# Turning blocks without TensorE: VectorE 32x32 transposes and GpSimd block copies in a hybrid attention layer

## The reference

```
h = rms_norm(x); proj = h @ w_in
retention (4 heads):      scores = (q k^T) * decay; o = scores v + (q * decay) (state from the chunk before)
gated delta rule (6):     short convolution, l2 norm, chunked triangular solve
attention (6 heads):      q, k normalised; softmax(q k^T - slope * distance) v, causal
y = concat over heads of rms_norm(o) * silu(gate)   (attention: o * silu(gate))
out = x + y @ w_out
```

## Time and profile before

| | before |
|---|---|
| median of 3 runs | 522.1 us (521.22 to 522.24) |
| profiled execution | 521.48 us |
| its span | 519.7 us |
| PE busy | 513.7 us (99%) |
| PEld (weight loads) | 431.3 us (83%) |
| DVE busy | 337.0 us (65%) |
| ACT busy | 277.0 us (53%) |
| POOL busy | 91.7 us (18%) |
| granted TensorE clock | 1.00 throughout |

### The profile page before, as it was taken

The page is one execution under the profiler, slowest core; times in us unless marked ns, Lnnn a source line. Parts: engine busy times, 40 slices in busy tenths (PEclk is TensorE's granted clock), DMA queues, the critical chain, the costliest instruction groups (busy, mean ns, idle before and its releaser), DMA issues.

```text
span 519.7 us, 8821 instructions
## 1 busy us (share of the span) xinstructions
PE 513.7 (99%) x3496; PEld 431.3 (83%) x3496; DVE 337.0 (65%) x529; ACT 277.0 (53%) x439; POOL 91.7 (18%) x84
## 2 busy tenths in 40 slices
PE   8999999999999999999999999999999999999996
PEld 6888888888888888888888888888888888888885
DVE  3999999989765876664644554655366455646551
ACT  5777645654356676565535554664556456443340
POOL 4764253316131312110000000100010010000000
PEclk9999999999999999999999999999999999999999
DMA  8999655765744466576676577657765557758711
GB/s 281 311 293 238 165 138 149 193 154 147 197 124 125 124 160 155 131 202 163 162 186 179 131 212 189 171 160 191 188 178 163 164 158 223 220 177 226 247 40 41
DMA packets 146923, 91.68 MB, mean 176 GB/s; under 512 B 7907, under 2 KB 135874, under 8 KB 146882
## 3 DMA queue, kind: packets, MB, share of 16 engines
q1 hardware_dynamic: 143392, 88.94, 63.0%
q10 hardware_dynamic: 3490, 2.18, 1.5%
HBM read 89.00 MB, written 2.10 MB: 175 GB/s over the span
## 4 chain that ended last, share of the span: by engine, by line
PE 97%; DVE 2%; ACT 0%; issue 0%; POOL 0%; DVEq 0%; POOLq 0%
PE pj L1450 20%; PE pj L1449 20%; PE pj L1447 20%; PE pj L1425 13%; PE pj L1426 6%; PE pj L1495 3%; PE pj L1504 1%; PE mx L1593 1%; PE pj L1422 1%; PE mx L1644 1%; DVE w_lo L353 1%; PE mx L1626 1%; PE mx L1474 1%; PE mx L1714 1%; PE pj L1512 1%; PE mx L1702 1%
## 5 line engine op out<-in xcount | busy, mean ns | idle before, releaser
L353 DVE TENSOR_TENSOR w_lo<-w_raw,w_hi 128x1024 fp32r<-128x1024 f32 x160 | 199.8, 1255 | 92.8 <-ACT w_hi L451 92.5
L451 ACT ACTIVATE w_hi<-w_raw 128x1024 fp32r<-128x1024 f32 x159 | 167.7, 1058 | 135.2 <-PE pj L1450 113.6
L1447 PE MATMUL pj<-w_hi,hT 128*128 128x512 f32 x320 | 127.4, 398 | 0.0
L1449 PE MATMUL pj<-w_hi,hT 128*128 128x512 f32 x320 | 125.9, 393 | 0.0
L1450 PE MATMUL pj<-w_lo,hT 128*128 128x512 f32 x320 | 124.9, 390 | 0.0
L1425 PE MATMUL pj<-hT,w_hi 128*128 128x512 f32 x300 | 109.3, 404 | 0.2 <-DVE w_lo L353 0.2
L1426 PE MATMUL pj<-hT,w_lo 128*128 128x256 f32 x300 | 83.9, 280 | 0.0
L1450 PEld LDWEIGHTS pj<-w_lo,hT 128*128 128x128 f32 x320 | 60.1, 188 | 12.4
L1447 PEld LDWEIGHTS pj<-w_hi,hT 128*128 128x128 f32 x320 | 60.1, 188 | 11.8
L1449 PEld LDWEIGHTS pj<-w_hi,hT 128*128 128x128 f32 x320 | 60.2, 188 | 11.3
L1425 PEld LDWEIGHTS pj<-hT,w_hi 128*128 128x128 f32 x300 | 56.3, 188 | 14.3 <-DVE w_lo L353 1.6
(11 more groups left out here) (241 smaller groups left out, 507.2 us busy)
## 6 DMA issues: line engine op xcount, KB each, us to landing
w_raw<-in_w_in_dram SPq DMA_DIRECT2D x256, 256.0 KB, 3.4
w_raw<-in_w_out_dram SPq DMA_DIRECT2D x64, 256.0 KB, 4.0
big<-in_x_dram SPq DMA_DIRECT2D x9, 256.0 KB, 5.5
out_dram<-sq ACTq DMA_DIRECT2D x7, 256.0 KB, 5.7
big<-in_x_dram SPq DMA_DIRECT2D x3, 512.0 KB, 7.2
cst<-table_dram SPq DMA_DIRECT2D x1, 682.0 KB, 9.8
big<-in_x_dram SPq DMA_DIRECT2D x2, 128.0 KB, 2.6
out_dram<-sq ACTq DMA_DIRECT2D x1, 128.0 KB, 2.4
```

What stands on the lines that cost most here:

```text
L353: eng.tensor_tensor(w_lo[:, n % NSPLIT, :], w_raw[:, n % NRAW, :], w_hi[:, n % NSPLIT, :].bitcast(F32), ALU.subtract).then_inc(S("lo"), 1)
L451: act.activation(w_hi[:, n % NSPLIT, :], w_raw[:, n % NRAW, :], ACT.Copy).then_inc(S("hi_done"), 1)
L1447: ins = pe.matmul(bank[:, :], src[:, kc, 0, tok], hi[:, k, :], start=first, stop=False)
L1449: pe.matmul(bank[:, :], src[:, kc, 1, tok], hi[:, k, :], start=False, stop=False)
```

## The change

The PE transposes of retention's k and q, of attention's q and of the output rows are removed (attention's keys and the gated delta rule's stay on PE). In their place a 128x512 tile is turned in two steps. DVE's transpose turns every 32x32 block where it stands; then POOL moves the blocks between the four 32-partition bands, by `move_blocks`: 16 copies of 32 partitions x (4 x 32) elements, in four groups of four, with a wait for all copies so far between groups. The temporary tiles `turned`, `spread` and `k_turned` lie in `mT`, which nobody reads any more. `r_kT`, `r_qT`, `m_qT` and `otr` count the last group's four copies. Retention's positions behind the turning move: `gram` from 14 to 42, `s1` 20 to 47, `o` 28 to 54, `out` 52 to 78. The splits of the output rows stand 20 (ACT) and 22 (DVE) units behind `out` where they stood two, and read `spread` in SBUF where they read PSUM. Three waits and counters are renamed (`m_nrm`, `m_alibi` become `m_step`).

```diff
-U_RET = {"tr": 6, "gram": 14, "s1": 20, "o": 28, "out": 52}
-U_MOBA = {"qtr": 5, "ktr": 26, "score": 34, "pt": 54, "o": 62, "out": 72}
+U_RET = {"gram": 42, "s1": 47, "o": 54, "out": 78}
+U_MOBA = {"ktr": 26, "score": 34, "pt": 54, "o": 62, "out": 72}
@@ ACT
-                advance(U["tr"] + 2)
-                act.wait_ge(S("r_tr"), j + 1)
-                act.activation(qT, mx[0][:, :], ACT.Copy).then_inc(S("r_qT"), 1)
...
-                advance(U["qtr"] + 2)
-                act.wait_ge(S("m_qtr"), j + 1)
-                act.activation(qT, mx[3][:, :], ACT.Copy).then_inc(S("m_qT"), 1)
...
-                advance(U["out"] + 2)
+                advance(U["out"] + 20)
@@ POOL
+            def spread_rows(p):
+                pool.wait_ge(S("y_turned"), p + 1 - FIRST_ROWS)
+                if p > FIRST_ROWS:
+                    pool.wait_ge(S("yt_lo"), p - FIRST_ROWS)
+                move_blocks(spread, turned, "otr")
+
+            def move_blocks(dst, src, done):
+
+                for d in range(4):
+                    if d:
+                        pool.wait_ge(S("moved"), moved[0])
+                    for q in range(4):
+                        a, i = q * QUART, (q ^ d) * QUART
+                        ins = pool.tensor_copy(dst[i:i + QUART, :, a:a + QUART], src[a:a + QUART, :, i:i + QUART])
+                        if d < 3:
+                            ins.then_inc(S("moved"), 1)
+                            moved[0] += 1
+                        else:
+                            ins.then_inc(S(done), 1)
...
                 power(64, 80, 8).then_inc(S("m_pow"), 1)
+                pool.wait_ge(S("m_pow"), j + 1)
+                pool.wait_ge(S("m_qtr"), j + 1)
+                pool.wait_ge(S("o_psum"), p)
+                move_blocks(four(qT), turned, "m_qT")
...
                 elif kind == "ret":
+                    pool.wait_ge(S("o_psum"), p)
+                    pool.wait_ge(S("y_lo"), GDN // 2)
+                    pool.wait_ge(S("r_tr"), 2 * j + 1)
+                    move_blocks(four(kT), k_turned, "r_kT")
+                    pool.wait_ge(S("r_tr"), 2 * j + 2)
+                    move_blocks(four(qT), turned, "r_qT")
                     rms_power(p)
+                    spread_rows(p)
                 else:
                     mix_moba(p, j, 128 * (p + 1))
+                    spread_rows(p)
@@ DVE
+            def turn_rows(p):
+                dve.wait_ge(S("on"), p + 1)
+                if p > FIRST_ROWS:
+                    dve.wait_ge(S("otr"), FIRST_ROWS + 4 * (p - FIRST_ROWS))
+                dve.transpose(turned.rearrange("p n c -> p (n c)"), on[:, :, :, :].rearrange("p h c e -> p (h c e)")).then_inc(S("y_turned"), 1)
...
-                advance(U["tr"] + 2)
-                dve.wait_ge(S("r_tr"), j + 1)
-                dve.tensor_copy(kT, mx[1][:, :]).then_inc(S("r_kT"), 1)
+                advance(base + 2)
+                dve.wait_ge(S("ev_done"), TOK_EV + in_rows(p))
+                if p > FIRST_ROWS:
+                    dve.wait_ge(S("otr"), FIRST_ROWS + 4 * (p - FIRST_ROWS))
+                for i, dst in ((1, k_turned), (0, turned)):
+                    dve.transpose(dst, both[:, :, i, :]).then_inc(S("r_tr"), 1)
...
                 dve.tensor_scalar(sm[:, 80:88], sm[:, 118:126], 1.0 / P, EPS, ALU.mult, ALU.add).then_inc(S("m_norm"), 1)
+                dve.wait_ge(S("otr"), FIRST_ROWS + 4 * (p - FIRST_ROWS))
+                dve.transpose(turned, both[:, :, 0, :]).then_inc(S("m_qtr"), 1)
                 gate(p)
...
-                advance(U["out"] + 2)
+                turn_rows(p)
+                advance(U["out"] + 22)
@@ PE
-                for i, bank in ((1, mx[1]), (0, mx[0])):
-                    for n in range(4):
-                        ins = pe.transpose(bank[:, n * P:(n + 1) * P], rows[n // 2][:, n % 2, i, :], ident)
-                ins.then_inc(S("r_tr"), 1)
-                stream(U["gram"])
-                pe.wait_ge(S("r_qT"), j + 1)
-                pe.wait_ge(S("r_kT"), j + 1)
+                pe.wait_ge(S("r_kT"), 4 * j + 4)
+                pe.wait_ge(S("r_qT"), 4 * j + 4)
...
-                for n in range(4):
-                    ins = pe.transpose(mx[3][:, n * P:(n + 1) * P], rows[n // 2][:, n % 2, 0, :], ident)
-                ins.then_inc(S("m_qtr"), 1)
...
-                pe.wait_ge(S("m_qT"), j + 1)
+                pe.wait_ge(S("m_qT"), 4 * j + 4)
...
-                stream(U["out"])
-                out_transposes(p, mx[3])
```

More of the change, by code:

```diff
@@ L272, in layer @@
         rows = [both[:, 2 * h:2 * h + 2] for h in range(2)]
+        FIRST_ROWS = GDN // 2
+        turned = mT[:, 0:4, :]
+        spread = mT[:, 4:8, :]
+        k_turned = mT[:, 8:12, :]
         kT = kq[:, 0].rearrange("p c k t -> p (c k t)")
@@ L720, in split_rows @@
             def split_rows(p, y0, scales):
-                act.wait_ge(S("otr"), p + 1)
+                act.wait_ge(S("otr"), FIRST_ROWS + 4 * (p + 1 - FIRST_ROWS))
                 if len(scales) == 1:
-                    act.activation(yT[:, y0:y0 + 2, 0, :], mx[3][:, :].rearrange("p (h t) -> p h t", h=2), ACT.Copy,
+                    act.activation(yT[:, y0:y0 + 2, 0, :], spread.rearrange("p (h c) t -> p h (c t)", h=2), ACT.Copy,
                                    scale=scales[0]).then_inc(S("yt_hi"), 2)
@@ L727, in split_rows @@
                     for h in range(2):
-                        act.activation(yT[:, y0 + h, 0, :], mx[3][:, h * T:(h + 1) * T], ACT.Copy, scale=scales[h]).then_inc(S("yt_hi"), 1)
+                        act.activation(yT[:, y0 + h, 0, :], spread[:, 2 * h:2 * h + 2, :].rearrange("p c t -> p (c t)"), ACT.Copy, scale=scales[h]).then_inc(S("yt_hi"), 1)
             def mix_ret(p, j, base):
@@ L858, in advance @@
                 pos[0] = max(pos[0], u)
+            def spread_rows(p):
[3 more added lines that the diff above has]
+                move_blocks(spread, turned, "otr")
+            moved = [0]
+            def move_blocks(dst, src, done):
[10 more added lines that the diff above has]
+                            ins.then_inc(S(done), 1)
             def rms_power(p):
@@ L1244, in split_rows @@
                 if len(scales) == 1:
-                    dve.scalar_tensor_tensor(yT[:, y0:y0 + 2, 1, :], mx[3][:, :].rearrange("p (h t) -> p h t", h=2), scales[0],
+                    dve.scalar_tensor_tensor(yT[:, y0:y0 + 2, 1, :], spread.rearrange("p (h c) t -> p h (c t)", h=2), scales[0],
                                              yT[:, y0:y0 + 2, 0, :].bitcast(F32), ALU.mult, ALU.subtract).then_inc(S("yt_lo"), 1)
@@ L1248, in split_rows @@
                     for h in range(2):
-                        ins = dve.scalar_tensor_tensor(yT[:, y0 + h, 1, :], mx[3][:, h * T:(h + 1) * T], scales[h],
+                        ins = dve.scalar_tensor_tensor(yT[:, y0 + h, 1, :], spread[:, 2 * h:2 * h + 2, :].rearrange("p c t -> p (c t)"), scales[h],
                                                        yT[:, y0 + h, 0, :].bitcast(F32), ALU.mult, ALU.subtract)
@@ L1283, in mix_moba @@
                     dve.wait_ge(S("m_sq"), 2 * j + h + 1)
-                    dve.tensor_reduce(sm[:, 118 + 4 * h:122 + 4 * h], sq[:, h].rearrange("p c k t -> p (c k) t"), AX.X, ALU.add).then_inc(S("m_nrm"), 1)
-                dve.wait_ge(S("m_nrm"), 2 * j + 2)
+                    dve.tensor_reduce(sm[:, 118 + 4 * h:122 + 4 * h], sq[:, h].rearrange("p c k t -> p (c k) t"), AX.X, ALU.add).then_inc(S("m_step"), 1)
+                dve.wait_ge(S("m_step"), 4 * j + 2)
                 dve.tensor_scalar(sm[:, 80:88], sm[:, 118:126], 1.0 / P, EPS, ALU.mult, ALU.add).then_inc(S("m_norm"), 1)
+                dve.wait_ge(S("otr"), FIRST_ROWS + 4 * (p - FIRST_ROWS))
+                dve.transpose(turned, both[:, :, 0, :]).then_inc(S("m_qtr"), 1)
                 gate(p)
@@ L1296, in mix_moba @@
                     dve.wait_ge(S("m_lg"), 4 * j + 2 * h + 2)
-                    dve.scalar_tensor_tensor(lg[:, h, :], cst[:, K_DIST:K_DIST + 3 * P], slope, lg[:, h, :], ALU.mult, ALU.add).then_inc(S("m_alibi"), 1)
-                    dve.wait_ge(S("m_alibi"), 2 * j + h + 1)
+                    dve.scalar_tensor_tensor(lg[:, h, :], cst[:, K_DIST:K_DIST + 3 * P], slope, lg[:, h, :], ALU.mult, ALU.add).then_inc(S("m_step"), 1)
+                    dve.wait_ge(S("m_step"), 4 * j + h + 3)
                     for c in range(C):
@@ L1719, in mix_ret @@
                 after_gdn = PAIRS[p - 1][0] == "gdn"
-                stream(U["tr"])
+                stream(U["gram"])
                 pe.wait_ge(S("ev_done"), TOK_EV + in_rows(p))
@@ L1755, in mix_moba @@
                 pt = [kT, qT]
-                stream(U["qtr"])
+                stream(U["ktr"])
                 pe.wait_ge(S("ev_done"), TOK_EV + in_rows(p))
                 pe.wait_ge(S("yt_lo"), p - GDN // 2)
-                for n in range(4):
-                    ins = pe.transpose(mx[3][:, n * P:(n + 1) * P], rows[n // 2][:, n % 2, 0, :], ident)
```

(2 more changed lines are left out.)

## The result

| | before | after |
|---|---|---|
| median | 522.17 us (4 runs) | 538.85 us (4 runs) |
| ratio to before | | 1.0323 (95%: 1.0298 to 1.0348) |
| profiled execution, its span | 521.48, 519.7 us | 539.85, 538.1 us |
| mean granted TensorE clock | 1.000 | 0.981 |
| POOL busy | 91.7 us | 180.2 us |

A forecast was written before the change was run, and what follows sets the result against it. PE was taken to bound the kernel, 99% busy and waiting for nobody: 521.5 - 5.3 us of transposes + 0.9 of attention's waits = 517.1 us profiled, 517.7 for the median; range 515.8 to 534.

The forecast's parts named there:

- What bounds the kernel, and what PE gets back: All changed stages: PE bounds the time, and removing its transposes gives 5.3 us if no wait arises.
- ACT and DVE cost nothing; the output rows are hidden: Weight splits and output moves: DVE's 9 us more is covered by the splits' lead; output moves hide behind weight matmuls.
- Do the four copies of a group overlap?: POOL's moves: with overlap a group takes 0.53 us and a move of 16 copies 2.1; without, 4.0 us.
- What a POOL copy costs: Each copy in POOL's moves: 0.37 us as recorded, 0.23 us start to start, 0.39 at the upper end.
- the rival in a row: POOL's moves: copies one after the other, behind w_lo where due; 6.7 us slower, 528.8; chance 0.26 for 523 to 535.
- POOL and DVE shut each other out: POOL against DVE: a w_lo (1.2 us) and a POOL operation that meet run one after the other.
- Retention's room: Retention's k and q before gram: 10.4 us of room, 4.2 for w_lo, 6.2 for POOL; 2.0 to spare with overlap.
- Attention's q: Attention's q before score: 5.9 us needed of 6.3 with overlap; 0.3 us a pair charged, 0.9 in all.
- what would show it: PE's waits and POOL's timeline: right if four copies within 0.6 us; wrong if gram or score wait microseconds for POOL.

The follow-up runs named there:

- The output rows alone: The changed kernel with retention's and attention's turning back on TensorE at the old positions, only the output rows turned by VectorE and GpSimd: 520.08 us, ratio 0.9954.
- the filler: The changed kernel with 32 further identity transposes on TensorE ahead of retention's gram and 24 ahead of attention's score: 532.06 us, ratio 1.0190.

## Why the prediction was wrong

*What bounds the kernel, and what PE gets back*: right. The output rows alone gave 2.1 of 2.2 us, and without waits the whole gain came in, 6.2 against 5.3.

*ACT and DVE cost nothing; the output rows are hidden*: right. No wait of PE for w_lo in the mixing stages, in any run.

*Do the four copies of a group overlap?* **This is the step that failed.** The forecast took two tiny memsets that started 0.03 us apart as a model for copies of different bands, and 2.1 us for a move, 0.13 a copy. The copies start 0.345 us apart, none inside another, so a move is 5.5 us when nothing holds it. Why they don't overlap stays open: each of them also raises a semaphore, and no run has them without. The Trainium skill's rule (GPSIMD Engine Reference, section Instruction dispatch), by which a core begins the next instruction when its own share is done, gave 2.1 us as well; no pair of copies in these traces shows it, and 5.5 was measured.

*What a POOL copy costs*: its recorded length lay inside the bounds, 0.29 us against a middle of 0.37. What was mis-sized is the distance between starts. I had made it shorter than the recorded length, 0.23; it is longer, 0.345, as 0.06 us pass between two copies. So the rival in a row, 528.8 us, was too mild as well, and the measured value went near its upper end of 0.39. The time fell where the prediction had put 0.12, beyond 535; by waits and transposes alone, without the clock, it would have been 531.2, inside the range and near the rival.

*POOL and DVE shut each other out*: right, also in that each copy takes its turn alone, a w_lo between any two. By that, and not by the copies' price alone, the moves became late: retention had 12.5 us of room for 11.0 us of copies and got 4.9 of w_lo in between.

*Retention's room*: I had put the transposes behind w_lo at 232.56 and the first copy at 234.6. That w_lo belongs to the next tile; the transposes came ahead of it and the first copy began at 232.27, so the room was larger by over 2 us, and five w_lo fell in it, not 3.5. Late by 3.5 us a pair, against nothing forecast and 1.8 in the rival.

*Attention's q*: the start (3.3 us behind the start of the square sums, as forecast) and the order of DVE's five operations were as described; the move took 9.04 us against the forecast's 5.9. Late by 2.6 us a pair, against 0.3 and the rival's 2.8.

*What was missing*: PE at 1.2 GHz after a wait. With 14.3 us of waits and 5.3 gained the sum is 9.0 us slower; 16.7 were measured, and the filler gave 6.8 of the other 7.7 back. So the prediction's last words, that it fails nowhere but on the copy's price or the order of turns, were wrong by these 7.7 us, nearly half of the loss. The Trainium skill has the rule (TensorE: Matmul & The Clock Gate, What's actually happening): an idle stretch drops the clock to half. Row and rule agree, 0.50 granted after 3.5 us of idleness, though not every wait of over 2 us was followed by it; and no term of the prediction charged a wait with it.

The signs named in "what would show it" told the two cases apart at one look: one copy each 0.35 us with holes of 1.0 us where w_lo runs.

## What to carry to other kernels

Price a helper engine's instruction by start-to-start distance of instructions like it, and don't let a saving hang on an overlap that no row shows. Where that engine meets another at a port, add the other's operations that fall in the room, near their full length (here 1.0 us for each w_lo of 1.23). When work goes off the bounding engine behind a deadline, sum the queue against that deadline first: here 12 of 32 and 8 of 16 copies on a third engine turned 16.7 us lost into 6.2 won. A wait of TensorE of some us can be dearer than its length, because of the clock behind it.

## What the runs showed that I had not expected

Copies of 32 partitions between different bands cost GpSimd 0.29 us and 0.06 to the next; ScalarE does four of them in 1.30 us, also with w_lo beside them. A 128x1024 operation of VectorE with one input took 0.7 us instead of 1.23, and held GpSimd's copies up by some 0.4. Waits of up to 0.7 us left the clock at 1.00; waits of 2.3 to 3.5 us were mostly, not always, followed by 3.4 or 6.8 us at 0.50, and that length sets the price.
